# Two norms per token tile shared by VectorE and ScalarE, three tile splits moved to VectorE, four table loads placed early

## The chip, the cores and the metric

The kernel runs on one core of a Trainium2 chip. The metric is the device time of one execution in microseconds (us), taken as the median of several. The core has five engines that run their own instruction streams and meet only at semaphores: TensorE (PE, matmuls and transposes into PSUM), VectorE (DVE), ScalarE (ACT), GpSimd (POOL) and SyncE (SP), which here only issues weight loads by DMA.

## The reference

Two transformer blocks on 256 tokens of width 1024, float32. What matters here are the places where a residual stream `x` is normalised, and what follows each.

```python
# block 1
x = layer_norm(ALPHA * x + g1 * mix) * ln1_g + ln1_b
h = layer_norm(x) * (1.0 + sc2) + sh2
ffn = moe_ffn(h, ...)        # router: sigmoid scores, top 8 of 64 experts; 38 expert steps
x = layer_norm(ALPHA * x + g2 * ffn) * ln2_g + ln2_b
# block 2, two layers
h = _rmsnorm(x, mix_norm[0]); x = x + _fox_pool_mixer(h, ...)
x = x + _swiglu(_rmsnorm(x, ffn_norm[0]), ...)
h = _rmsnorm(x, mix_norm[1]); x = x + _rwkv7_time_mix(h, ...)
x = x + _swiglu(_rmsnorm(x, ffn_norm[1]), ...)
```

## The kernel before

The 256 tokens are two tiles of 128 partitions (`NT = 2`, t = 0 and 1). `x` and `h_tok` hold both as 128 x 2 x 1024. Weights come as 1 MB tiles of 128 x 2048 through a ring of 6 slots, issued in order by SP (L588); each load waits until PE has used the slot's last tile. A product is done in three float32r matmuls (L809 to L811): ACT rounds a tile to its high part (`round_tile`, L1598, semaphore `w_hi`), and DVE or POOL subtracts it to get the rest in `ring_lo` (`rest_of_tile` on DVE, L2075; `rest_of_tiles` on POOL, L638; semaphore `w_split`). Only then may PE use the tile.

The order on every engine is the order of the program text, written out by hand. `Steps` makes an instruction wait for the one ahead of it on its own engine. What an engine waits for it waits for in order, so an instruction behind a wait is late with it.

Norms: `layer_norm` (L2035) and `rms_norm` (L2044) on DVE take bn_stats of two halves and bn_aggr per token tile, ask ACT for the square roots of both tiles at once (`root(2)`, L1626 to L1630, semaphores `root_asked` and `root_done`), take the reciprocal (L2016), and scale both tiles (L2042, or L2051 and L2052). An affine `x * gain + bias` runs over both tiles at once (L2348, L2349 after `w_o`, L2467, L2468 after the experts). Then PE transposes `h_tok` (`turn_all`, `turn_half`, L890), ACT writes the high part of the transposed rows (`hT_parts`, L1615 or L1618), and DVE the rest (L2098 or L2101). The stages named after the transposes are h2T (into the router), a0T (first mixer), f0T (first feed-forward), r0T (second mixer) and f1T (second feed-forward).

Router: PE multiplies by `router_w` (`stack`, L874), ACT copies the partial sums (`stacked_sums`, L1624), PE adds them (`stack_sums`, L863), ACT takes the Sigmoid (L1828) after it has rounded the last of the three tiles of the shared expert ("moe", 2), and DVE sorts out the top 8 (L2361 to L2385). POOL makes the rests of the three "moe" tiles. `placed` on DVE then works out which expert sits where (L2124 to L2166); at its first `tables` (L2141) POOL issues the first indirect loads of expert weights (L705, L709), and later gathers the tokens' rows of `h2_rows` (L697). `mod_gate_half` (L2068) copies the gate of the second half to SBUF on DVE. `routed` on PE runs the 38 expert steps (L1041 transposes, L1055 gate and up, L1074 down, L1088 combine).

## Time and profile before

| | |
|---|---|
| runs (us) | 1967.17, 1970.4, 1979.52; median 1970.4 |
| profiled execution | 1973.28 us, of it 1971.5 us from first to last instruction |
| PE busy | 1778.5 us (90%), granted clock 0.947 on average |
| DVE / ACT / POOL busy | 930.2 / 644.8 / 519.9 us |
| chain that ended last | PE 76%, DVE 11%, DMA 7%, ACT 3%, issue 3%, POOL 1% |

The chain that ended last is followed back from the last instruction, at each step to what released it. So DVE is busy for 47% of the time but only 11% of the span hangs on it. Most of that 11% lies in the short stretches between two products, where a norm must be finished before PE has work again. All times below are us from the start of the span, unless marked otherwise.

### The profile page before, as it was taken

To read this page: it belongs to the slowest core of one execution; us is meant where nothing else is said; L and a number is where in the kernel's file an instruction comes from. 1 tells how busy PE (TensorE), PEld (TensorE's weight loads), DVE (VectorE), ACT (ScalarE), POOL (GpSimd) and SP (SyncE) were. 2 spreads that over 40 slices of the span, in tenths; PEclk is the share of its full clock that TensorE was granted. 3 is DMA by queue.
4 is the path that set the end of the run, shared out by engine and by line. 5 is a ranking of instruction groups with operands and counts; after the bars stand their busy time and mean duration, and the time that the engine had idled before them with its cause. 6 is when DMAs were issued, how large, how long until landed. Compare 5 with 4: busy or idle time off the path is not lost.

```text
span 1971.5 us, 29696 instructions
## 1 busy us (share of the span) xinstructions
PE 1778.5 (90%) x12406; PEld 1277.0 (65%) x12406; DVE 930.2 (47%) x1355; ACT 644.8 (33%) x863; POOL 519.9 (26%) x372
## 2 busy tenths in 40 slices
PE   5989998999779999999999498889997979979998
PEld 2889996795534344444444276678886749857887
DVE  4286626677612121222222664455447765665453
ACT  3444345241202111111111234343434352324442
POOL 0278888100434445354543000000000002200000
PEclk9999999899879999999999688889998989989999
DMA  9445551167599998979897432155553400023442
GB/s 360 179 150 193 181 185 42 65 237 283 221 423 423 416 384 312 390 295 397 329 380 311 180 128 86 64 187 192 191 190 133 168 22 25 3 70 143 183 183 104
DMA packets 64970, 414.40 MB, mean 210 GB/s; under 512 B 20613, under 2 KB 20629, under 8 KB 24529
## 3 DMA queue, kind: packets, MB, share of 16 engines
q0 software_dynamic: 37808, 218.05, 27.5%
q1 hardware_dynamic: 26624, 192.95, 26.4%
q8 instruction: 92, 1.51, 0.3%
q10 hardware_dynamic: 416, 1.66, 0.2%
q14 instruction: 30, 0.24, 0.0%
HBM read 550.99 MB, written 2.10 MB: 281 GB/s over the span
## 4 chain that ended last, share of the span: by engine, by line
PE 76%; DVE 11%; DMA 7%; ACT 3%; issue 3%; POOL 1%; DVEq 0%; POOLq 0%; ACTq 0%; SPq 0%
PE ps L1055 12%; PE ps L809 10%; PE ps L810 10%; PE ps L811 10%; PE ps L1074 6%; PE ps L845 4%; PE ps L846 4%; PE ps L847 4%; PE ps L1088 3%; PE ps L1413 2%; PE ps L863 1%; PE ps L1041 1%; DMA ring<-in_moe_dn,arena 1%; DMA arena<-in_moe_dn,arena 1%; PE ps L1449 1%
## 5 line engine op out<-in xcount | busy, mean ns | idle before, releaser
L810 PE MATMUL ps<-ring_lo,arena_r 128*128 128x512 f32 x888 | 356.0, 401 | 0.0
L1055 PE MATMUL ps<-arena 128*32 128x512 f32 (+2 forms) x832 | 244.4, 601 | 7.5 <-DMA spare<-in_moe_gu,arena 3.9
L809 PE MATMUL ps<-arena_r 128*128 128x512 f32 x528 | 211.4, 400 | 7.0 <-DVE arena_r L2101 7.0
L847 PE MATMUL ps<-arena_r,ring_lo 128*128 128x256 f32 x768 | 215.7, 281 | 0.0
L811 PE MATMUL ps<-arena_r 128*128 128x512 f32 x528 | 207.7, 393 | 0.0
L1055 PE MATMUL ps<-ring,arena 128*32 128x512 f32 (+2 forms) x560 | 201.5, 601 | 4.9 <-issue 2.1
L810 PEld LDWEIGHTS ps<-ring_lo,arena_r 128*128 128x128 f32 x888 | 171.4, 193 | 35.6
L2075 DVE TENSOR_TENSOR ring_lo<-ring,arena_r 128x2048 fp32r<-128x2048 f32 x66 | 150.7, 2291 | 77.6 <-ACT arena_r L1598 77.5
L638 POOL TENSOR_TENSOR ring_lo<-ring,high 128x2048 fp32r<-128x2048 f32 x28 | 128.5, 4591 | 132.9 <-ACT high L1598 132.9
L1598 ACT ACTIVATE high<-ring 128x2048 fp32r<-128x2048 f32 x62 | 118.4, 1917 | 125.1 <-PE ps L845 67.7
L845 PE MATMUL ps<-arena_r,high 128*128 128x256 f32 x528 | 151.3, 287 | 3.0 <-DVE ring_lo L2075 1.4
L2446 DVE SCALAR_TENSOR_TENSOR arena<-ps,arena 128x256 f32<-128x256 f32 x38 | 18.4, 484 | 277.4 <-ACT arena L1699 277.4
L846 PE MATMUL ps<-arena_r,high 128*128 128x256 f32 x528 | 149.1, 282 | 0.0
L847 PEld LDWEIGHTS ps<-arena_r,ring_lo 128*128 128x128 f32 x768 | 145.7, 190 | 0.0
L1598 ACT ACTIVATE arena_r<-ring 128x2048 fp32r<-128x2048 f32 x66 | 126.1, 1919 | 38.6 <-DMA ring<-in_weights 38.6
L1055 PEld LDWEIGHTS ps<-arena 128*32 128x32 f32 (+2 forms) x832 | 75.6, 126 | 77.9 <-issue 77.8
L1074 PE MATMUL ps<-arena 128*32 128x512 f32 (+2 forms) x416 | 123.9, 596 | 0.5 <-ACT arena L1707 0.5
L890 PE MATMUL ps<-cst,arena 128*128 128x128 f32 x372 | 63.4, 318 | 65.9 <-DVE arena L2052 34.1
L1055 PE MATMUL ps<-spare,arena 128*32 128x512 f32 (+1 forms) x272 | 121.5, 600 | 0.6
L809 PEld LDWEIGHTS ps<-arena_r 128*128 128x128 f32 x528 | 100.2, 190 | 27.2 <-issue 7.6
L811 PEld LDWEIGHTS ps<-arena_r 128*128 128x128 f32 x528 | 100.2, 190 | 21.3
L845 PEld LDWEIGHTS ps<-arena_r,high 128*128 128x128 f32 x528 | 100.1, 190 | 6.8 <-issue 2.7
(451 smaller groups left out, 3559.5 us busy)
## 6 DMA issues: line engine op xcount, KB each, us to landing
ring<-in_weights SPq DMA_DIRECT2D x183, 1024.0 KB, 4.8
arena<-in_ln POOLq DMA_DIRECT2D x2, 1024.0 KB, 7.5
arena<-in_lora POOLq DMA_DIRECT2D x1, 1152.0 KB, 5.5
arena<-in_x POOLq DMA_DIRECT2D x1, 1024.0 KB, 12.7
h_rows<-arena ACTq DMA_DIRECT2D x1, 1024.0 KB, 11.0
arena<-in_bands POOLq DMA_DIRECT2D x1, 1024.0 KB, 11.8
arena<-in_rw_kk_ka POOLq DMA_DIRECT2D x2, 512.0 KB, 7.3
arena<-in_rw_w0a POOLq DMA_DIRECT2D x1, 1024.0 KB, 4.8
```

The source lines that it names most:

```text
L638: pool.tensor_tensor(ring_lo[:, s, :], ring[:, s, :], hi_of(stage, i).bitcast(F32), ALU.subtract).then_inc(sem(f"w_split{s}"), 1)
L809: head = pe.matmul(dst, hi, w, start=start, stop=False, skip_group_check=True)
L810: pe.matmul(dst, hi, rest, start=False, stop=False, skip_group_check=True)
L811: return head, pe.matmul(dst, lo, w, start=False, stop=stop, skip_group_check=True)
L845: head = pe.matmul(dst, w, hi[:, k, :], start=(k == 0), stop=False)
L846: pe.matmul(dst, w, lo[:, k, :], start=False, stop=False)
L847: mm = pe.matmul(dst, rest, hi[:, k, :], start=False, stop=(k == count - 1))
L890: mm = pe.transpose(pb(stage, unit)[0:src.shape[1], n * P:n * P + src.shape[0]], src, ident)
L1055: mm = pe.matmul(pb("moe", mu("gu", i))[at, :], x_cols[:, k, at], gu_w[s % SETS][:, k * 512:(k + 1) * 512], start=(k == 0), stop=(k == KC ...
L1074: mm = pe.matmul(pb("moe", mu("y", i, n))[at, :], hid_cols[:, i % 2, f, at], dn_w[s % SETS][:, f * D + n * 512:f * D + n * 512 + 512], sta ...
L1598: fn(hi_of(stage, i), ring[:, s, :], ACT.Copy).then_inc(sem(f"w_hi{s}"), 1)
L2075: tt(ring_lo[:, s, :], ring[:, s, :], hi_of(stage, i).bitcast(F32), S).then_inc(sem(f"w_split{s}"), 1)
```

## The change

- The norms go by token tile. After `w_o` and after the experts, DVE asks for tile 0's root as soon as its moments are known (`ask_deviation`), ACT takes it (`root(1, t)`), DVE writes 1/deviation and -mean/deviation (`centre`), and ACT normalises the tile in place with one ACTIVATE with a scale and a bias per partition (`centred_rows`, semaphore `scaled`). Gain, bias and moments run on DVE per tile (`norm_with_gain`).
- Of each following norm into `h_tok`, ACT scales tile 0 (`scaled_rows`) and DVE tile 1 (`rms_of_second`). PE transposes tile 0 as soon as ACT has it (`turn_tile(stage, 0)`), tile 1 after DVE. This holds for a0T, f0T, r0T and f1T; h2T is turned as before.
- The rests of the three "moe" tiles leave POOL for DVE, tiles 0 and 1 ahead of the top-8 search and tile 2 behind it, ahead of `placed`. The copies of `mod_gate` go from DVE to ACT.
- ACT rounds tile ("moe", 2) after the router's Sigmoid. The rest of ("hy_in", 1) moves on DVE from ahead of the norm after the experts to behind it, and ACT rounds ("hy_in", 0) one step earlier.
- `warm(func)` is an ACTIVATE on one column. It makes the compiler put the table load of `func` there: Sigmoid at the router, Exp ahead of the copies of `qkT`, Tanh, Sigmoid and Exp in the second mixer.

```diff
 @@ POOL
             row(buf(7), a["ln1"]).then_inc(sem("ln_in"), 16)
-            rest_of_tiles("moe", 3)
 @@ PE (the same for f0T, r0T, f1T with scaled 7, 8, 9)
+            pe.wait_ge(sem("scaled"), 6)
+            turn_tile("a0T", 0)
             pe.wait_ge(sem("a0_ready"), 1)
-            turn_all("a0T", h_tok, KC)
+            turn_tile("a0T", 1)
 @@ ACT
+            def centred_rows(t):
+                scales[0] += 1
+                act.wait_ge(sem("scale_ready"), scales[0])
+                fn(x[:, t, :], x[:, t, :], ACT.Identity, bias=sml("ms", 1, t),
+                   scale=sml("rs", 1, t)).then_inc(sem("scaled"), 1)
+            def scaled_rows(shifted=False):
...
+                    ins = fn(h_tok[:, 0, :], x[:, 0, :], ACT.Copy, scale=sml("rs", 1))
+                ins.then_inc(sem("scaled"), 1)
+            def warm(func):
+                step(fn(sml("warm", 1), sml("one", 1), func))
...
+                round_tile("hy_in", 0)
                 y_rounded(STEPS - 1)
-                round_tiles("hy_in", 0, 1)
+                round_tile("hy_in", 1)
...
+            root(1, 0)
+            centred_rows(0)
             partial_sums("ada2", 0)
-            root(2)
-            partial_sums("ada2", 1, 2)
-            root(2)
+            root(1, 1)
+            centred_rows(1)
+            partial_sums("ada2", 1)
+            root(1, 0)
+            scaled_rows(shifted=True)
+            partial_sums("ada2", 2)
+            root(1, 1)
             partial_sums("ada2", 3)
...
             stacked_sums("router")
-            round_tile("moe", 2)
+            warm(ACT.Sigmoid)
+            for u in range(2):
+                full(act, "gate2", 2 * u + 1)
+                step.read(fn(mod_gate[:, u * 512:(u + 1) * 512], pb("gate2", 2 * u + 1), ACT.Copy), "gate2", 2 * u + 1)
             for t in range(NT):
                 full(act, "router", 1 + t)
                 step.read(fn(rt_scores[:, t, :], pb("router", 1 + t)[:, 0:EXPERTS], ACT.Sigmoid), "router", 1 + t)
+            round_tile("moe", 2)
...
-            root(2)
+            root(1, 0)
+            scaled_rows()
+            root(1, 1)
             hT_parts("f0T", p2("ffn_norm", 8))
 @@ DVE
+            def norm_with_gain(gain, bias, name, ask, answer):
+                for t in range(NT):
+                    scaled_seen[0] += 1
+                    dve.wait_ge(sem("scaled"), scaled_seen[0])
+                    step(tt(x[:, t, :], x[:, t, :], gain, M))
+                    if t == 0:
+                        centre(1)
+                    else:
+                        answer()
+                        scaled_seen[0] += 1
+                    step(tt(x[:, t, :], x[:, t, :], bias, A), name if t else None)
+                    for half in range(2):
+                        half_moments(x, t, half)
+                    if t == 0:
+                        ask(0)
...
             hT_parts("h2T")
-            for u in range(2):
-                mod_gate_half("gate2", u, u)
+            rest_of_tiles("moe", 0, 1)
...
             step(tt(flat(picked), above, masked, ALU.not_equal), "marks")
+            rest_of_tile("moe", 2)
             experts("moe")
...
-            rest_of_tiles("hy_in", 0, 1)
+            rest_of_tile("hy_in", 0)
...
-            rms_norm(h_tok, x, "a0_ready")
+            norm_with_gain(buf(0)[:, 0:D], buf(0)[:, D:2 * D], "x2_ready", ask_rms, rms_of_first)
+            rms_of_second("a0_ready")
+            rest_of_tile("hy_in", 1)
```

How the instructions stand on ACT at the router, before: the row of L1624 is just ahead of these.

```order
L1598 ACTIVATE twin_r<-ring 128x2048 [waits w_loaded2,ps_read3]
L1828 ACT_TABLE_LOAD
L1828 ACTIVATE arena<-ps 128x64 [waits ps_full4]
L1828 ACTIVATE arena<-ps 128x64 [waits ps_full5,ps_read4]
L1637 ACT_TABLE_LOAD [waits gu_full0]
L1637 ACTIVATE arena<-ps 128x256 [waits ps_read5]
```

And of the change, on the same engine and place (its own line numbers: L1672 is `warm`, L1877 the copies of `mod_gate`, L1880 the Sigmoid, L1617 the rounding, L1679 the Silu of the shared expert):

```order
L1672 ACT_TABLE_LOAD
L1672 ACTIVATE small<-small 128x1 [waits ps_read3]
L1877 ACTIVATE arena<-ps 128x512 [waits ps_full4,act_order]
L1877 ACTIVATE arena<-ps 128x512 [waits ps_full6,ps_read4]
L1880 ACTIVATE arena<-ps 128x64 [waits ps_full4,ps_read6]
L1880 ACTIVATE arena<-ps 128x64 [waits ps_full5,ps_read4]
L1617 ACTIVATE twin_r<-ring 128x2048 [waits w_loaded2,ps_read5]
L1679 ACT_TABLE_LOAD
L1679 ACTIVATE arena<-ps 128x256 [waits gu_full0]
```

The Sigmoid no longer stands behind the rounding that waits for the weight tile, and the Silu's table load no longer carries the wait for PE.

On DVE between the last expert step and the first moments, before (L2433 ends the last step's masks, L2461 is the first work on the experts' sum):

```order
L2433 TENSOR_SCALAR last_r<-arena 128x128 x2
L2075 TENSOR_TENSOR ring_lo<-ring,high 128x2048 [waits w_hi3]
L2075 TENSOR_TENSOR ring_lo<-ring,high 128x2048 [waits w_hi4]
L2461 TENSOR_TENSOR arena<-ps,arena 128x512 [waits combined]
L2461 TENSOR_TENSOR arena<-ps,arena 128x512 [waits dve_order]
```

The same place in the change:

```order
L2540 TENSOR_SCALAR last_r<-arena 128x128 x2
L2177 TENSOR_TENSOR ring_lo<-ring,high 128x2048 [waits w_hi3]
L2570 TENSOR_TENSOR arena<-ps,arena 128x512 [waits combined,ps_read6,ps_read4]
L2570 TENSOR_TENSOR arena<-ps,arena 128x512 [waits dve_order]
L2573 SCALAR_TENSOR_TENSOR arena<-arena 128x1024 [waits dve_order]
```

One of the two rests has left this place; it stands behind `a0_ready` now.

## Rows read from the trace of the kernel before

**Rows 1.** The waits of PE: engine line waited for, us in total, times, longest.
```profile
PE ps L890 <- DVE arena L2052: 34.1, 3, 25.0
```

**Rows 2.** Stretches: PE, PEld, DVE, ACT, POOL busy (x count), granted clock, DMA share, GB/s.
```profile
545.00:559.00 14.00, 2.81 (x14) 2.66 (x14) 0.40 (x2) 0.00 (x0) 3.95 (x4) 0.50 1.01 421
559.00:1101.00 542.00, 527.32 (x3179) 239.76 (x3177) 114.94 (x231) 100.67 (x192) 229.05 (x232) 0.99 0.91 364
```

**Rows 3.** DVE's timeline behind `w_o`: start, us, line, form, idle before and releaser.
```profile
472.32 0.69 DVE L2343 TENSOR_TENSOR arena<-ps,arena 128x512 f32<-128x512 f32 x1 [0.41 <-PE ps L811]
488.17 1.23 DVE L2061 SCALAR_TENSOR_TENSOR arena<-ps,arena 128x1024 f32<-128x1024 f32 x1
```

**Rows 4.** ACT's timeline at the router and the shared expert.
```profile
501.34 0.38 ACT L1624 ACTIVATE arena<-ps 128x256 f32<-128x256 f32 x1
503.67 1.91 ACT L1598 ACTIVATE twin_r<-ring 128x2048 fp32r<-128x2048 f32 x1 [1.94 <-DMA ring<-in_weights]
505.60 1.28 ACT L1828 ACT_TABLE_LOAD   x1
516.08 1.28 ACT L1637 ACT_TABLE_LOAD   x1 [8.71 <-PE ps L811]
```

**Rows 5.** DVE's timeline in the top-8 search.
```profile
507.46 1.31 DVE L2361 TENSOR_TENSOR arena<-arena 128x128 f32<-128x128 f32 x1 [3.45 <-ACT arena L1828]
508.81 3.23 DVE L2363 MAX8 arena<-arena 128x8 f32<-128x8 f32 x16
512.08 1.17 DVE L2364 TENSOR_TENSOR arena<-arena 128x16 f32<-128x16 f32 x1
513.29 0.29 DVE L2372 TENSOR_TENSOR arena<-arena 128x128 f32<-128x128 f32 x1
```

**Rows 6.** POOL's timeline: the three rests, then the first load of expert weights.
```profile
499.62 9.00 POOL L638 TENSOR_TENSOR ring_lo<-ring,high 128x2048 fp32r<-128x2048 f32 x2 [50.47 <-ACT high L1598]
508.59 4.62 POOL L638 TENSOR_TENSOR ring_lo<-ring,twin_r 128x2048 fp32r<-128x2048 f32 x1
523.14 1.06 POOL L705 DMA_INDIRECT ring<-in_moe_gu,arena  x1 [9.93 <-DVE arena L2141]
```

**Rows 7.** The chain that ended last, at the gather: start, us, what.
```profile
541.09 17.32 DMA arena<-h_rows,arena
558.46 1.97 PE ps L1041 x8
```

**Rows 8.** DVE's timeline behind the experts.
```profile
1099.60 4.49 DVE L2075 TENSOR_TENSOR ring_lo<-ring,high 128x2048 fp32r<-128x2048 f32 x2 [0.72 <-ACT high L1598]
1104.01 1.41 DVE L2461 TENSOR_TENSOR arena<-ps,arena 128x512 f32<-128x512 f32 x2
1115.23 2.29 DVE L2467 TENSOR_TENSOR arena<-arena 128x2048 f32<-128x2048 f32 x1
1125.23 0.75 DVE L2052 TENSOR_SCALAR arena<-arena,small 128x1024 f32<-128x1024 f32 x1
```

**Rows 9.** DVE behind `hy_out`, then ACT at f0T and at the second mixer.
```profile
1280.55 0.69 DVE L2547 TENSOR_TENSOR arena<-ps,arena 128x512 f32<-128x512 f32 x1 [1.15 <-PE ps L811]
1284.21 0.75 DVE L2052 TENSOR_SCALAR arena<-arena,small 128x1024 f32<-128x1024 f32 x1
...
1286.23 3.22 ACT L1618 ACTIVATE arena_r<-ps,small 128x256 fp32r<-128x256 f32 x8 [3.11 <-PE ps L890]
...
1498.20 1.06 ACT L1901 ACTIVATE arena_r<-arena 128x1024 fp32r<-128x1024 f32 x1 [3.69 <-DVE arena L2588]
```

**Rows 10.** DVE's timeline behind r0T.
```profile
1489.85 1.22 DVE L2572 TENSOR_TENSOR arena<-arena 128x1020 f32<-128x1020 f32 x1 [0.83 <-ACT arena L1588]
```

**Rows 11.** ACT's timeline at two table loads for Exp, and the copies ahead of one.
```profile
1200.99 2.49 ACT L1581 ACTIVATE arena<-ps 128x512 f32<-128x512 f32 x4
1207.54 1.28 ACT L1870 ACT_TABLE_LOAD   x1 [4.06 <-DVE small L2515]
...
1603.03 1.28 ACT L1934 ACT_TABLE_LOAD   x1 [6.47 <-DVE arena L2633]
```

117 lines of the change are left out of this document (90 added, 27 removed).

## Prediction

> **What bounds the kernel now.** I read the busy shares first, then the waits of PE, then the chain that ended last, and then the timelines of DVE, ACT and POOL in each stretch that the diff touches. PE is busy for 90% of the span, so only stretches in which PE has nothing to do can pay. In the 38 expert steps it has almost none: 527 us of matmuls in 542 us at full clock, with the DMA engines 91% busy beside it [rows 2]. That stretch should move as a block. PE's largest wait is for the second scaling of a norm, 34.1 us in three waits, 25.0 of them behind the experts [rows 1]. The changed stretches are eight: `w_o` to the router, the router to the first gather, the experts' end to a0T, the attention's start, f0T, r0T, the Exp in the second mixer, and f1T. The sum is made stretch by stretch, against the profiled execution of 1973.28 us. It lies 2.9 us above the median of the runs, 1970.4.
>
> **Prices.** A DVE instruction costs its duration and about 0.03 us. A 128 x 2048 tensor_tensor takes 2.29 us [rows 8], half of it 1.22 [rows 10], a tiny one about 0.2 with its gap (estimate: the 0.29 of 128 elements [rows 5] less its length). No instruction before normalises 1024 columns on ACT. Its nearest row is a plain Copy of 1024 columns, 1.06 us [rows 9]. Above, the bound is the 1.91 us of a 2048 column rounding [rows 4]. I take 1.06, since the shape is the same. DVE does a tile in 0.75 [rows 8].
>
> **1. `w_o` to the router: 0.7 us.** Before, the modulation of `ada2` starts at 488.17, 15.85 us after the last product piece at 472.32 [rows 3]. In the new order DVE loses two whole-tile scalings per norm half to ACT and one exposed root, but gains 5 tiny instructions. Walked through by the prices, the modulation starts at 486.4, 1.8 us earlier. Not all of it gets through. ACT must round the weight tiles ("moe", 0) and ("moe", 1) ahead of `stacked_sums`, and the tile after them is only there at 503.67, after ACT had waited 1.94 us for it [rows 4]. Loads come back to back here, so tile 1 is about one load and half the `h2_rows` store earlier, near 499, and its rounding ends near 500.8. `stacked_sums` then starts at about 500.7 and not at 501.34 [rows 4], which leaves 0.6 to 0.7. Bounds: 0 if the tile is later, 1.8 if not in the way.
>
> **2. The router: 3.0 us more.** Before: rounding from 503.67 to 505.58, table load to 506.88, two Sigmoids, DVE starts at 507.46 [rows 4, 5]. New: `stacked_sums` ends at 501.1, load 1.28, warm 0.2, two gate copies of 0.6 (the chained 0.62 of a 512 column copy [rows 11]), Sigmoids 0.5: DVE starts at 504.5, so 2.96 earlier, the 0.7 of step 1 among it. Then DVE's two small tensor_tensors took 1.31 and 1.17 us where the same form with 128 elements takes 0.29. The first ended at 508.77 and the second at 513.25, when POOL's rests ended at 508.62 and 513.21 [rows 5, 6]. The 16 MAX8, with one input each, were not held. With the rests gone from POOL, I credit 1.0 and 0.9. Bounds 0 and 1.9. So the search ends 4.9 us earlier. Against that, the rest of ("moe", 2), 2.29 us like L2467 [rows 8], stands ahead of `placed`. Before, DVE sat about 1 us here until PE had counted. PE itself starts the shared expert 2.9 us earlier. `placed` starts 3.7 us earlier by this: 2.96 + 1.9, less 2.3, plus the 1 us of sitting and 0.1. The Silu's load (1.28 behind a wait of 8.71 [rows 4]) now lies in the slack and pays nothing, as the rest covers it. If that rest were quicker, it would pay up to 1.3.
>
> POOL's first indirect load, at 523.14, waits for DVE L2141 [rows 6], which is in `placed`. The gather is issued at 541.09 and its rows land 17.3 us later, at 558.4 [rows 7], with the DMA full at 421 GB/s [rows 2]: it lies behind four sets of expert weights. Hence it lands 3.7 us earlier exactly if the first load is issued 3.7 us earlier. **Steps 1 and 2: 3.7 us** of the start of the expert steps.
>
> **3. Behind the experts: 4.0 us.** PE's last combine ends at 1101.04 (the modelled end). DVE starts on it only at 1104.01, behind two rests from 1099.60 [rows 8]. With one rest left it starts at 1101.2: 2.8. From there to `a0_ready` it was 21.97 us (1104.01 to 1125.98 [rows 8]). By tile: two products and a scaling of x 2.72, moments 1.70, ask 0.2, products 1.46, centre 0.4, 1.26, 1.70, 0.2; then gain 1.26, centre 0.4, bias 1.26, 1.70, 0.4; 1.26, 0.2, 1.26, 1.70; 0.4, root 0.3, reciprocal 0.2, scaling 0.78. Together 20.8: 1.2 saved. The norm saves so little because two scalings, 1.7 us, and one exposed root, 0.8, leave DVE, while the splitting adds tiny instructions. PE has turned tile 0 meanwhile. Unit 0 of a0T is complete two transposes after `a0_ready` instead of four, about 0.45 at low clock; but the moved rest, 2.3 us, delays DVE's half of a0T by that much again. With it in between, DVE's half comes about as much later as the earlier transposes bring, so the 0.45 is not counted. Total 2.8 + 1.2 = 4.0.
>
> **4. Attention: 0.2 us lost.** The load at 1207.54 sat behind a wait of 4.06 and was exposed, 1.28. But the warm Exp now stands ahead of the four `qkT` copies, which run back to back from 1200.99 [rows 11] and which PE waits for. It costs 1.28 and 0.2 there. The load is moved from one place on the path to another.
>
> **5. f0T and f1T: 1.3 us each.** The last piece starts at 1280.55, `f0_ready` is at 1284.96, ACT's first hT at 1286.23 [rows 9]. New: 0.72, reciprocal 0.2, 0.73, 0.24, 0.4, root 0.3, 0.2, 0.78 gives `f0_ready` at 1284.15, 0.8 earlier; ACT's tile 0 is done at 1282.6. Unit 0 needs two transposes less after it, 0.45. With `f1_ready` the rows repeat. **r0T: 0.3**, since the rounding of ("rw_r", 2) and its rest still lie ahead of L2572, which waited only 0.83 for ACT [rows 10].
>
> **6. Exp in the second mixer: 1.3 us.** The load at 1603.03 is exposed behind a wait of 6.47 [rows 11]. ACT is idle ahead of it, so warming hides all 1.28. The loads for Tanh and Sigmoid are not waited for: the products behind them wait for a later one.
>
> Sum: 3.7 + 4.0 - 0.2 + 2.6 + 0.3 + 1.3 = **11.7 us**, 1973.3 becomes 1961.6, and the median 1970.4 becomes **1958.7**.
>
> The Trainium skill (ScalarE: Activation LUTs, What ACT_TABLE_LOAD costs) adds a drain and puts each switch at about 2.66 us. By it step 6 would be worth 2.66 and step 4 would still about cancel, a sum of 13.1 and 1957.3. The trace shows the next ACTIVATE right behind the 1.28, so I keep 1.28. The same page (Rules for kernel authors) sends adds and multiplies to VectorE, against this change. By it ACT's tile would be the last one, which is the third rival.
>
> **The rivals.**
> - Forecast, chance 0.60: 1958.7, own range 1955 to 1963 (step 1 from 0 to 1.8, the port from 0 to 1.9, each step's latencies).
> - The router's gain stays out, 0.18. The search is sooner, but `placed` is held by the rest of ("moe", 2), or that tile lands later as the `h2_rows` store now shares its DMA time. For: DMA full until 503.7, 2.29 us ahead of `placed`. Against: 5 us between its landing and its use. Steps 1 and 2 give 0 to 1: 11.7 - 3.2 = 8.5, 1961.9.
> - ACT's tile is the last, 0.10. If a per-partition ACTIVATE of 1024 takes the upper bound, 1.91, it is 0.85 longer. There are eight such on ACT, and at about four of them DVE has no work of its own left to cover it: 3.4 lost, 1962.1.
> - Slower, 0.04: PE's clock. It was granted at half before the first gather, 0.50 [rows 2], after PE had sat idle. If at the six restarts it stays at the low level (1.2 GHz) longer, every us of it costs half a us of matmuls. It decides from 23 us more of low clock, 4 us per restart. With 8 us per restart it would be 24 - 11.7 = 12.3 slower: 1982.7. Against: the gaps get shorter, not longer.
> - Large gain, 0.05: the waits in the expert steps, 14.7 us of 542 [rows 2], shrink with the new phase of loads by 8 or more: 1950.
> - It changes nothing, 0.03: every gain is given back in the 14.7 us of waits: 1970.
>
> **How the numbers follow.** 1% is 19.7 us, about what a measurement of this kernel can tell from no change. Only the large gain with all else at its upper bound passes it, and the clock must take 31 us to pass on the other side. Faster 0.05, same 0.92, slower 0.03. The forecast, the router's and ACT's rivals hold 0.88. The range over them, widened for the runs' own scatter (the median lies 3 above the lowest run, 9 below the highest), is 1952 to 1967.5.
>
> **What would show it.** In the changed profile: the first Sigmoid at about 504, not 506.9; L2361's and L2364's counterparts at 0.3 each; POOL's first indirect load near 519.4; PE's first expert transposes near 554.7; DVE's first work on the experts' sum within 0.3 us of PE's end; `a0_ready` 20.8 us after it; first ACT hT at f0T 4.4 us after the last piece, not 5.7; the Exp at the second mixer with no load ahead; `qkT` copies 1.5 us later. It is wrong if the small tensor_tensors stay at 1.2 without POOL, if an ACTIVATE of 1024 takes 1.5 or more, or if the expert steps take longer than 542 us.

## The result, and the profile after

The changed kernel takes 1957.46 us (median of 17 runs), the kernel before 1970.49 us beside it. The ratio is 0.9933, with a 95% interval from 0.9919 to 0.9948: 13.2 us less, between 10.2 and 16.0. The forecast was 11.7 us less and 1958.7 us. The profiled execution spans 1955.7 us, 15.8 less than the 1971.5 of before.

So the number came out. The reasons did so only in part, and the stages show where. The table cuts the span at marks that every kernel here has (an instruction on DVE, or the first matmul of a product on PE), so each row is the difference of two start times read from the timelines. "Last piece" is the last tensor_tensor in which DVE adds a product's result.

| stretch (us) | before | change | difference | forecast |
|---|---|---|---|---|
| start to the last `w_o` piece (unchanged code) | 472.32 | 476.22 | +3.90 | 0 |
| to the first tensor_tensor of the top-8 search | 35.14 | 34.01 | -1.13 | -3.0 |
| to `placed` | 11.19 | 10.09 | -1.10 | -0.7 |
| to PE's first expert transposes | 39.81 | 39.99 | +0.18 | 0 |
| to PE's last combine | 542.19 | 538.43 | -3.76 | 0 |
| to DVE's first work on the experts' sum | 3.36 | 0.53 | -2.83 | -2.8 |
| to PE's first matmul behind a0T | 28.73 | 27.48 | -1.25 | -1.2 |
| to the last q/k piece on ACT | 67.62 | 66.63 | -0.99 | 0 |
| attention, to the last `hy_out` piece | 80.19 | 75.95 | -4.24 | +0.2 |
| f0T, to the first product | 11.58 | 10.33 | -1.25 | -1.3 |
| to the feed-forward's last piece | 190.05 | 189.35 | -0.70 | 0 |
| r0T, to the first product | 14.16 | 13.08 | -1.08 | -0.3 |
| to DVE's last LoRA sums (L2633) | 105.90 | 106.87 | +0.97 | 0 |
| the Exp, to DVE's next instruction | 7.23 | 5.94 | -1.29 | -1.3 |
| to the last `rw_o` piece | 157.68 | 156.45 | -1.23 | 0 |
| f1T, to the first product | 11.31 | 10.31 | -1.00 | -1.3 |
| to the end | 193.04 | 194.04 | +1.00 | 0 |

Six rows (the experts' end, the norm behind it, f0T, r0T, the Exp, f1T) hold little but work that the change moved, and sum to 8.7 us. The two rows at the router (to the search and to `placed`) are the change's too, 2.2 us more. The largest rows, +3.90, -3.76 and -4.24, lie where I had forecast nothing or next to nothing. Whether the code makes them, one pair of profiles can't tell.

The page of the changed kernel: busy times, and three groups of PE's waits (engine line, releaser: us in total, times, longest). Compare [rows 1].

```profile
PE 1774.3 (91%) x12406; PEld 1270.9 (65%) x12406; DVE 929.4 (48%) x1370; ACT 657.8 (34%) x886; POOL 506.5 (26%) x369
```

```profile
PE ps L904 <- ACT arena L1667: 22.1, 3, 17.5
PE ps L861 <- ACT arena L1877: 3.5, 1, 3.5
PE ps L904 <- DVE arena L2135: 3.0, 3, 1.5
```

The wait of 25.0 us behind the experts has become 17.5 us for ACT's tile 0 and 1.5 for DVE's tile 1. The second row is new: PE's router sums (L861) wait 3.5 us for ACT's copy of `mod_gate`.

ACT's timeline at the router in the change (start, us, line, form, idle before and releaser), to be held against [rows 4].

```profile
500.54 1.91 ACT L1617 ACTIVATE high<-ring 128x2048 fp32r<-128x2048 f32 x1 [0.90 <-DMA ring<-in_weights]
504.32 1.91 ACT L1617 ACTIVATE high<-ring 128x2048 fp32r<-128x2048 f32 x1 [1.87 <-DMA ring<-in_weights]
506.14 0.37 ACT L1643 ACTIVATE arena<-ps 128x256 f32<-128x256 f32 x1
506.52 1.28 ACT L1672 ACT_TABLE_LOAD   x1
508.05 1.23 ACT L1877 ACTIVATE arena<-ps 128x512 f32<-128x512 f32 x2
509.55 0.22 ACT L1880 ACTIVATE arena<-ps 128x64 f32<-128x64 f32 x1 [0.27 <-PE ps L861]
```

The Sigmoid no longer waits for tile ("moe", 2), but it waits for tile ("moe", 1). Here and below a tile counts as landed when ACT starts to round it. That is 28.1 us behind the last `w_o` piece (504.32 less 476.22). Then the load, the warm instruction and the first copy stand ahead of PE's sums.

DVE's timeline in the change: the search, and the stretch behind the experts. Compare [rows 5, 8].

```profile
510.23 0.29 DVE L2467 TENSOR_TENSOR arena<-arena 128x128 f32<-128x128 f32 x1 [1.67 <-ACT arena L1880]
510.55 3.24 DVE L2469 MAX8 arena<-arena 128x8 f32<-128x8 f32 x16
513.83 0.19 DVE L2470 TENSOR_TENSOR arena<-arena 128x16 f32<-128x16 f32 x1
...
1099.27 1.42 DVE L2570 TENSOR_TENSOR arena<-ps,arena 128x512 f32<-128x512 f32 x2
...
1119.28 0.75 DVE L2135 TENSOR_SCALAR arena<-arena,small 128x1024 f32<-128x1024 f32 x1
1120.06 2.29 DVE L2177 TENSOR_TENSOR ring_lo<-ring,high 128x2048 fp32r<-128x2048 f32 x1
1122.27 4.11 DVE L2203 SCALAR_TENSOR_TENSOR arena_r<-ps,small,arena_r 128x256 fp32r<-128x256 f32 x8
```

The two small tensor_tensors take 0.29 and 0.19 us, not 1.31 and 1.17. Behind the experts `a0_ready` falls at 1120.03, which is 20.76 us after DVE's start at 1099.27. The forecast had 20.8.

### The profile page after: what moved, and what is told of

Read it like the earlier page. It is cut to its first block, busy times and chain, and to the rows that moved or that the text cites. A ratio compares the mean times of both kernels' runs of the same rounds, so it can differ in the third digit from the quotient of the medians.

```text
span 1955.7 us, 29751 instructions
## 1 busy us (share of the span) xinstructions
PE 1774.3 (91%) x12406; PEld 1270.9 (65%) x12406; DVE 929.4 (48%) x1370; ACT 657.8 (34%) x886; POOL 506.5 (26%) x369
## 3 DMA queue, kind: packets, MB, share of 16 engines
q1 hardware_dynamic: 26624, 192.95, 26.7%
## 4 chain that ended last, share of the span: by engine, by line
PE 76%; DVE 11%; DMA 7%; issue 3%; ACT 3%; POOL 1%; DVEq 0%; POOLq 0%; ACTq 0%
PE ps L1066 12%; PE ps L807 10%; PE ps L808 10%; PE ps L809 10%; PE ps L1085 6%; PE ps L845 4%; PE ps L843 4%; PE ps L844 4%; PE ps L1099 3%; PE ps L1430 3%; PE ps L861 2%; PE ps L1052 1%; DMA ring<-in_moe_dn,arena 1%; DMA arena<-in_moe_dn,arena 1%; PE ps L1466 1%
## 5 line engine op out<-in xcount | busy, mean ns | idle before, releaser
L1617 ACT ACTIVATE high<-ring 128x2048 fp32r<-128x2048 f32 x62 | 118.6, 1916 | 128.4 <-PE ps L843 67.6
L638 POOL TENSOR_TENSOR ring_lo<-ring,high 128x2048 fp32r<-128x2048 f32 x26 | 119.6, 4604 | 82.8 <-ACT high L1617 82.8
L1617 ACT ACTIVATE arena_r<-ring 128x2048 fp32r<-128x2048 f32 x66 | 126.1, 1920 | 38.5 <-DMA ring<-in_weights 38.5
L2177 DVE TENSOR_TENSOR ring_lo<-ring,high 128x2048 fp32r<-128x2048 f32 x36 | 82.3, 2292 | 55.7 <-ACT high L1617 55.2
L1741 ACT ACTIVATE arena<-ps 128x256 f32<-128x256 f32 x38 | 14.6, 384 | 269.0 <-PE ps L1066 269.0
```

Source lines behind the costliest of these rows:

```text
L638: pool.tensor_tensor(ring_lo[:, s, :], ring[:, s, :], hi_of(stage, i).bitcast(F32), ALU.subtract).then_inc(sem(f"w_split{s}"), 1)
L1617: fn(hi_of(stage, i), ring[:, s, :], ACT.Copy).then_inc(sem(f"w_hi{s}"), 1)
L2177: tt(ring_lo[:, s, :], ring[:, s, :], hi_of(stage, i).bitcast(F32), S).then_inc(sem(f"w_split{s}"), 1)
```

## The experiments

All kernels are timed against the kernel before on the same chip. Ratios have a 95% interval. A difference of 1 to 3 us is below what a median tells here (the intervals are 5 to 16 us wide), so what a run decides is read from its stages. A granted clock of 1.00 is TensorE's 2.4 GHz, 0.50 is 1.2 GHz, called half clock here.

### What holds the router: copies of `mod_gate` back on DVE

```diff
 @@ ACT
-            for u in range(2):
-                full(act, "gate2", 2 * u + 1)
-                step.read(fn(mod_gate[:, u * 512:(u + 1) * 512], pb("gate2", 2 * u + 1), ACT.Copy), "gate2", 2 * u + 1)
 @@ DVE
-            rest_of_tiles("moe", 0, 1)
+            rest_of_tile("moe", 0)
+            for u in range(2):
+                mod_gate_half("gate2", u, u)
+            rest_of_tile("moe", 1)
```

> The changed kernel, but the two copies of mod_gate are made by DVE again, between the rests of tiles (moe, 0) and (moe, 1). Measure: from the last w_o piece on DVE to the first tensor_tensor of the top-8 search, 35.14 us before and 34.01 in the change, where I had forecast 32.2. Theory 1 (the copies hold the router): in the change PE's router sums wait 3.51 us for the second... the first copy of mod_gate on ACT, which stands behind the Sigmoid's table load (1.28) and the warm instruction (0.20), since both use one PSUM bank. With the copies on DVE the sums run beside the load, and the search starts when the load and the rest of (moe, 1) end: 1.6 us sooner, 32.4 us, and the first indirect load of POOL and PE's first expert transposes come sooner by 1.4 to 1.7. Theory 2 (only the landing of weight tile (moe, 1), 28.1 us behind the last w_o piece, holds the router): 34.0 again, nothing moves. Total: 1.5 us, below what five rounds can tell.

Measured: from the last `w_o` piece to the search 32.10 us, 1.9 less than in the change. From there to PE's expert transposes 50.1, as in the change. Ratio to the kernel before 0.9936 (0.9911 to 0.9960), so the total doesn't show it. PE's timeline of this kernel at the router sums and the shared expert:

```profile
502.36 0.66 PE L861 MATMUL ps<-cst,arena 128*128 128x64 f32 x4 [0.27 <-ACT arena L1643]
504.80 0.77 PE L807 MATMUL ps<-high,arena_r 128*128 128x512 f32 x1 [1.78 <-ACT arena L1877]
```

The sums wait 0.27 us for `stacked_sums` and no longer 3.51 for a copy behind the load. In the change that wait is in this row:

```profile
508.79 1.09 PE L861 MATMUL ps<-cst,arena 128*128 128x64 f32 x4 [3.51 <-ACT arena L1877]
```

Theory 1 holds: my forecast had priced the two copies as 1.2 us of ACT time, and not seen that they stand behind the table load on PE's way to the Sigmoid. But not all of the 1.9 us are the copies', since tile ("moe", 1) came 1.0 us sooner in this profile (27.1 us behind the last `w_o` piece, not 28.1). Counted from that tile's rounding, the search starts 5.6 to 6.0 us later in the five kernels with the copies on ACT. With the copies on DVE and a tile as late (28.0 and 29.6 us, two kernels below) it starts 4.2 us later, which is ACT's 1.91 and DVE's 2.29 for that tile. So the copies are worth 1.4 to 1.7 us where the tile is late.

### DVE and POOL: rests back on POOL, and rests on DVE in the kernel before

```diff
 @@ POOL
+            rest_of_tiles("moe", 3)
 @@ DVE
-            rest_of_tiles("moe", 0, 1)
...
-            rest_of_tile("moe", 2)
```

> The changed kernel, but POOL makes the rests of the three moe tiles again. Measure: the two small tensor_tensors of the top-8 search, 1.31 and 1.17 us before, 0.29 and 0.19 in the change. Theory 1 (DVE and POOL hold each other up): POOL's rests run beside the search, and one or both take over 1 us again, where a rest runs beside them; the MAX8 between them stay at 3.2 for 16. Theory 2 (something else of the change made them short, such as the place of the Sigmoid): 0.3 and 0.2. The first indirect load moves little either way: 2 us of such delays against 2.29 us of the rest of (moe, 2) which no longer stands ahead of placed.

Ratio 0.9958 (0.9935 to 0.9981), median 1963.75. From the last `w_o` piece to PE's expert transposes it took 87.5 us, where four profiles with the change's router took 83.8 to 85.1: on the mean 1.3 more up to the search, since the weight tile came late (29.7 us), and 1.8 more from there to `placed`. DVE's and POOL's timelines of this kernel:

```profile
508.16 1.34 DVE L2468 TENSOR_TENSOR arena<-arena 128x128 f32<-128x128 f32 x1 [12.52 <-ACT arena L1882]
509.53 3.23 DVE L2470 MAX8 arena<-arena 128x8 f32<-128x8 f32 x16
512.80 1.91 DVE L2471 TENSOR_TENSOR arena<-arena 128x16 f32<-128x16 f32 x1
```

```profile
500.38 8.97 POOL L638 TENSOR_TENSOR ring_lo<-ring,high 128x2048 fp32r<-128x2048 f32 x2 [51.03 <-ACT high L1619]
510.09 4.58 POOL L638 TENSOR_TENSOR ring_lo<-ring,twin_r 128x2048 fp32r<-128x2048 f32 x1 [0.75 <-ACT twin_r L1619]
```

Each held instruction ends 0.04 to 0.16 us after a POOL instruction: 509.50 after 509.35, 514.71 after 514.67. The MAX8 between, with one input, isn't held, though POOL's third rest starts beside it. How much is lost depends on the moment. In the kernel before with an early Exp (below), the third rest started 0.03 us ahead of the search. Its DVE and POOL timelines:

```profile
511.95 4.68 DVE L2366 TENSOR_TENSOR arena<-arena 128x128 f32<-128x128 f32 x1 [4.58 <-ACT arena L1832]
```

```profile
511.92 4.55 POOL L638 TENSOR_TENSOR ring_lo<-ring,twin_r 128x2048 fp32r<-128x2048 f32 x1
```

Here 0.29 us of work took 4.68, `placed` began 14.42 us after the search's start and not 11.19, and from `w_o` to PE's expert transposes it was 92.13 us, 6 more than the 86.14 of the first profile. Of these 6 us 3.2 lie between the search and `placed`, the others ahead of and behind it. So theory 1 of the experiment with POOL's rests holds: DVE and POOL hold each other up. The Trainium skill (SBUF — State Buffer, SBUF: two separate sides) says that VectorE and GpSimd share a port pair, and that of an instruction of VectorE with two SBUF inputs and one of GpSimd that reads SBUF, the one that starts first locks the other out for its whole length. By that rule, the traces agree: 0.64 to 4.68 us where POOL's rest was under way, 0.29 and 0.19 where it wasn't.

Then the same alone in the kernel before (tile 0's rest ahead of the `mod_gate` copies, tile 1's behind, tile 2's ahead of `placed`):

> The kernel before, with one thing of the change: DVE makes the rests of the three moe tiles, (0) ahead of the two copies of mod_gate, (1) behind them, (2) ahead of placed. In the profiles so far the first small tensor_tensor of the search took 1.31, 1.34 and 4.68 us and the second 1.17, 1.91 and 0.19 us wherever POOL made the rests (before, the change with POOL rests, before with the early Exp), and 0.29 and 0.19 wherever DVE made them; undoing the DVE rests in the change took the median from 1957.5 to 1963.8. Measure: the two durations, the time from the last w_o piece to PE's first expert transposes (86.1, 87.5 and 92.1 us in those three), and the median. Theory 1 (the delay by POOL is the larger part of what the router gives, and is larger on average than the 2.5 us of the profile of before): 0.3 and 0.2 us, the stage takes 84 to 86 us, and the median falls by 3 to 6 us. Theory 2 (my forecast: 1.9 us of delay against 2.29 us of the rest ahead of placed): the stage 85 to 86 us and the median the same within 1 us.

The two took 0.29 and 0.19 us, the stage to PE's expert transposes 86.62 us, against 86.14 and 86.66 in the two profiles of the kernel before in which the delay was small. Ratio 1.0000 (0.9975 to 1.0025). So theory 2: what the port gives back, the rest of ("moe", 2) ahead of `placed` takes. What remains is that the bad case of 92 can't occur. How often it occurs in the kernel before, three profiles don't tell.

### The attention: where the Exp's load stands

One place in the change, moved behind the copies:

```diff
 @@ ACT
-            warm(ACT.Exp)
             copy_units("qkT", 4, lambda i: buf(10)[:, i * 512:(i + 1) * 512])
+            warm(ACT.Exp)
```

> The changed kernel, but the warm Exp stands behind the four qkT copies instead of ahead of them. Measure: from the last q/k piece that ACT copies (L1913 of the change) to the last hy_out piece on DVE: 80.2 us before, 75.95 in the change, where I had forecast 80.4. Theory 1 (latency only): the copies start 1.48 us sooner and the load stays hidden in ACT's wait of about 5 us, so 74.5 us, and PE's wait ahead of the first logits is 1.7 instead of 3.2 us. Theory 2 (the clock decides): in the change the granted clock falls to half in PE's 3.2 us wait and is back 9 us later, before the loop over the heads is under way; before the change it stayed full there and fell in the next wait (2.4 us), and was half from 1209 to 1222.5. With the shorter first wait the fall comes later, inside the loop, and the stage is 76 to 79 us although the copies are sooner.

And in the kernel before, the warm Exp ahead of the copies, as the change has it:

> The kernel before, with one thing of the change: the warm Exp ahead of the qkT copies. Measure: from the last q/k piece that ACT copies to the last hy_out piece, 80.2 us before. Theory 1 (my forecast, latency only): the load moves from one place on the path to another, 80.4 us. Theory 2 (the clock): the wait of PE ahead of the first logits grows from 1.7 to 3.2 us, the clock falls there and is back before the loop over the heads is under way, and the stage takes about 76 us as in the change. If it takes 80, the 4.2 us came from something else of the change, or from chance.

Ratios: 0.9899 (0.9863 to 0.9936) for the late one in the change, 0.9983 (0.9959 to 1.0006) for the early one in the kernel before. The stage from the last q/k piece to the last `hy_out` piece, in all profiles of this study, with PE's busy time at half clock in it (windows of 2 us, PE's busy time in each times twice the share of the clock that was missing):

| Exp's load | stage (us) | of it half clock (us) |
|---|---|---|
| exposed in the loop (before, and two experiments on it) | 80.2, 75.6, 77.6 | 26.5, 15.9, 21.6 |
| ahead of the copies (change twice, three experiments on it, one on before) | 76.0, 77.6, 78.6, 76.0, 77.6, 77.5 | 17.8, 22.2, 22.9, 18.0, 22.0, 21.9 |
| behind the copies (five kernels) | 73.4, 73.1, 71.5, 73.5, 73.2 | 14.1, 16.3, 9.7, 14.0, 16.5 |

The stretches of the attention in three kernels, and in a fourth further down: PE, PEld, DVE, ACT, POOL busy (x count), granted clock, DMA share, GB/s. First the kernel before.

```profile
1200.99:1209.00 8.01, 4.89 (x26) 3.17 (x24) 2.80 (x7) 3.83 (x6) 0.00 (x0) 1.00 0.35 131
1209.00:1222.50 13.50, 12.48 (x39) 9.20 (x40) 4.96 (x16) 5.12 (x18) 0.00 (x0) 0.51 0.01 1
```

The change:

```profile
1195.52:1197.50 1.98, 0.00 (x0) 0.00 (x0) 0.00 (x0) 1.88 (x4) 0.00 (x0) 0.94 0.99 418
1197.50:1206.80 9.30, 8.55 (x21) 5.31 (x22) 2.74 (x7) 1.60 (x5) 0.00 (x0) 0.50 0.01 4
```

The change with the Exp behind the copies:

```profile
1190.81:1218.00 27.19, 22.48 (x128) 16.04 (x127) 15.61 (x46) 14.48 (x40) 0.00 (x0) 1.00 0.11 39
```

Before, the clock fell inside the loop over the heads, behind PE's wait for the exposed load. In the change it fell one wait sooner, where the warm Exp had made that wait 3.2 us instead of 1.7. With the load behind the copies both waits are short (1.7 and 1.1 us), and here the clock stays full for 27 us, into the loop. That is so in three of the five kernels with the late load. In the other two, the combined one and the last one below, the clock fell all the same, for 6.8 us from 5.2 and 5.5 us behind the last q/k piece, after the same 1.7 us of waiting. The combined kernel:

```profile
1198.50:1205.30 6.80, 6.80 (x19) 4.43 (x19) 3.14 (x8) 2.19 (x9) 0.00 (x0) 0.50 0.00 1
```

So with the short waits the first fall is spared or 6.8 us long, and the length of the waits alone does not settle which. In the kernels with the exposed or the early load it came each time and lasted 6.8 to 13.7 us.

So the -4.24 us of the first pair of profiles is not the early Exp's merit: means are 77.8 us where the load is exposed (75.6 to 80.2), 77.2 with the early warm (76.0 to 78.6), 72.9 with the late one (71.5 to 73.5). The first two can't be told apart, and the 77.5 of the early warm in the kernel before decides for neither theory of that run: it lies between its two values and among the others. The forecast of about nothing stands, for a reason that I had not named. My theory 2 of the late Exp (the fall comes later and costs more) is refuted, and theory 1 had the 1.5 us but not the 3 more of the clock. The relation is plain in the table: from 9.7 to 26.5 us of half clock the stage grows by 8.7, about half a us for each. The late load's gain shows in the total too: 0.9899 is the lowest ratio of any kernel here without the idle transposes of the last experiments.

### The experts' end: one rest moved in the kernel before

```diff
 @@ ACT
-                y_rounded(STEPS - 1)
-                round_tiles("hy_in", 0, 1)
+                round_tile("hy_in", 0)
+                y_rounded(STEPS - 1)
+                round_tile("hy_in", 1)
 @@ DVE
-            rest_of_tiles("hy_in", 0, 1)
+            rest_of_tile("hy_in", 0)
...
             rms_norm(h_tok, x, "a0_ready")
+            rest_of_tile("hy_in", 1)
```

> The kernel before, with one thing of the change: the rest of (hy_in, 1) stands behind the scaling into h_tok and no longer ahead of the merge of the experts' sum, and ACT rounds (hy_in, 0) a place earlier. Measure: from PE's last combine to DVE's first work on the sum (3.36 us before, counted from the start of the last matmul; 0.53 in the change), and from that to PE's first stack matmul behind a0T (28.7 before, 27.5 in the change). Theory (the forecast's step 3): 0.5 for the first, 2.8 us sooner; the second grows by the moved rest less what hid it, to 30.5 to 31, since here all of the transposes come behind a0_ready and DVE's half of a0T would stand right behind them; so of the 2.8 us 0.5 to 1 stay in the first product's start, if the rest is in the way, and all 2.8 if PE's 3.7 us of transposes cover it. This kernel has the attention of before unchanged: its stage from the last q/k piece to the last hy_out piece was 80.2 us in the one profile of before; if clock chance made that, it may come out between 76 and 80 here.

From PE's last combine to DVE's first work on the sum: 0.43 us instead of 3.36. From there to the first matmul behind a0T 28.69, and 28.72 to 28.74 in three profiles of kernels with both rests in the old place. So all of the 2.9 us stay, and the moved rest costs nothing behind `a0_ready`: PE needs 3.7 us for its transposes at half clock, and the 2.29 fit beside them. That part of my expectation (0.5 to 1 us lost) was wrong. The norm by tile, the rest of what the change does there, then gives the 1.25 us more, the same in every profile with it and the rest in this place (27.46 to 27.49). Ratio 0.9995 (0.9968 to 1.0022): a gain of 3 us that the median does not show.

### f1T: what the clock takes back

The norm ahead of f1T as before (one root for both tiles, both scalings on DVE, `turn_all`), all else as in the change.

> The changed kernel with the norm ahead of f1T as before: one root for both tiles, both scalings on DVE, all transposes behind it. Measure: from the last rw_o piece to the first product of the feed-forward (11.31 us before and 10.31 to 10.66 in the change), and from there to the end (192.8 to 193.0 before, 193.9 to 194.0 in the change). Theory 1 (the clock takes the gain back): PE's transposes by tile leave it at half clock 1.5 to 2 us longer in the feed-forward, so with this norm undone the first part is 11.3 and the second 193.0, and the sum is the same 204.3. Theory 2 (the feed-forward got slower for another reason of the change): 11.3 and 194.0, sum 205.3.

Ratio 0.9957 (0.9932 to 0.9982). f1T took 11.31 us and the rest to the end 193.49, the sum 204.8: between the theories. The first 8 us of the last feed-forward, in the kernel before, the change, and this one (columns as above, the clock is third from the end):

```profile
1778.46:1786.46 8.00, 8.00 (x28) 6.42 (x29) 4.24 (x3) 3.15 (x4) 0.00 (x0) 0.79 0.00 0
```

```profile
1761.66:1769.66 8.00, 8.00 (x24) 6.33 (x25) 3.90 (x2) 2.22 (x2) 0.00 (x0) 0.65 0.00 0
```

```profile
1769.71:1777.71 8.00, 8.00 (x26) 6.43 (x27) 4.03 (x2) 2.66 (x3) 0.00 (x0) 0.72 0.00 0
```

In 8 us the clock was half for 3.4, 5.6 and 4.5 us (twice the missing share). Take half a us of lost work for each from the time to the end: 193.04 less 1.7 is 191.3, 194.04 less 2.8 is 191.2, 193.49 less 2.25 is 191.2. The feed-forward itself is the same in all three, and the clock alone makes the difference. The kernels with a full clock there, below, bear it out: they take 191.3 us. So theory 1 is right about the cause. It is not right about the amount, since undoing the norm brought back half of it, not all. In the seven profiles with the norm by tile and no fill the sum of f1T and what follows is 204.2 to 204.6, in the four of the kernel before and what was made from it 204.0 to 204.4. Nothing is won at f1T. That the one profile with this norm undone lies 0.2 to 0.7 us above all of these is left open.

### Chance and code: the change again, and repairs together

> The changed kernel as it is, for a second profile and for the median beside the two below on one chip. If the stages are a matter of the code, from the last w_o piece to PE's first expert transposes it is 84 to 85 us, merge to the first product behind a0T 27.5, f0T 10.3, r0T 13.1, the Exp stretch of the second mixer 5.9, f1T 10.3 and behind it 193.9. What differs more than 0.3 us from the first profile (I expect the experts by up to 3 us, the attention by up to 3 us, and the start up to w_o by up to 8) is chance, and should go with the time at half clock in it.

Median 1962.3, ratio 0.9941 (0.9919 to 0.9963). The own stretches repeat within 0.06 us (27.49 behind the experts, 10.33 at f0T, 13.08 at r0T, 5.93 at the Exp, 10.37 at f1T) or 0.3 us (193.85 behind f1T, 83.8 from `w_o` to PE's expert transposes). Others do not. The experts took 541.4 us and not 538.4. The start up to `w_o` was 474.96 here and ranged from 468.3 to 476.3 over all profiles, with the same code in it. That scatter does go with the clock, as I had expected: TensorE was granted half clock for 13.7 us of the start in the three profiles of 468.3 to 468.5, and for 30.7 us in the five above 475.2. So the +3.90 of the first table is chance. The experts ranged from 538.0 to 544.3 in the change and the kernels made from it, and from 539.6 to 542.2 in the kernel before and those made from it. The two overlap, so the -3.76 is not shown to be the code's. With the clock it does not go: 538.4 and 541.4 us had 8.9 and 8.1 us at half.

Then three repairs together: the `mod_gate` copies on DVE, the Exp behind the copies, the rest of ("hy_in", 1) behind DVE's half of a0T.

> The changed kernel with three repairs: the copies of mod_gate on DVE, the warm Exp behind the qkT copies, and the rest of (hy_in, 1) behind DVE's half of a0T. From the profiles so far: 1.9 us at the router, 1.5 to 2.5 in the attention, and up to 0.6 at a0T, where DVE's half started 1122.27 with ACT's first two pieces done 0.5 to 0.6 us before. Theory 1 (the gains add up): 4 to 5 us under the change, a median near 1953. Theory 2 (only the attention counts, and the router's gain is lost in the loads of the expert steps): 1955.

Ratio 0.9912 (0.9882 to 0.9941), median 1955.44. The stages: 33.86 to the search (the weight tile landed late), 27.05 behind the experts (0.43 less), 73.1 in the attention. Behind the experts and in the attention the repairs hold by stage. At the router this profile has only 0.5 us of the 1.9 (83.9 us to PE's expert transposes against 84.4 in the change), but the two others with the copies on DVE and the last rest in its old place have 2.1 (82.2 and 82.4). The median is the 1955 of theory 2, yet the stages do not bear out its reason, that the router's gain is lost. By the ratios the total is 4 to 6 us better than the change's, with intervals that overlap, and no better than the late Exp's load alone (0.9899).

On top of it, the rest of ("moe", 2) inside `placed`:

```diff
-            rest_of_tile("moe", 2)
             experts("moe")
...
+                rest_of_tile("moe", 2)
                 dve.wait_ge(sem("slots"), 4)
```

> The combined kernel of the run before (mod_gate on DVE, warm Exp late, rest of (hy_in, 1) late), and DVE makes the rest of (moe, 2) inside placed, ahead of its wait for PE's fourth result (1.1 us), and no longer ahead of it. Theory 1 (the first indirect load sets when the tokens' rows land: from it to PE's first expert transposes it was 35.3 to 35.6 us in all nine profiles): PE counts at about 1.6 us behind the search's end, so placed starts 0.9 us sooner, and so do the first indirect load and the transposes: 83.0 us from the last w_o piece instead of 83.9, with 35.5 unchanged. Theory 2 (the gather's own issue, 18 us behind the first load and held by DVE, sets it): the rest delays DVE by 1.2 to 2.3 us in between, so the 35.5 grow to 36.5 to 37.5 and the stage is 84.2 to 85.

From search to `placed` 9.17 us instead of 10.07, from there to PE's expert transposes 39.8 and not longer: theory 1. Ratio 0.9918 (0.9889 to 0.9948), median 1955.96: the total doesn't tell it from the one before. On the same chip the change itself took 1962.3, so all the repairs together are worth 6.3 us there. Over all profiles it was 35.3 to 35.8 us from the first indirect load to the first expert transposes, whatever DVE did in between. The prediction's assumption that this time is fixed held.

### PE kept busy in its waits

If the time at half clock is what separates these kernels, then giving PE something to do should pay more than a faster norm. `fill` is so many transposes of the identity into a PSUM bank that nobody reads (shown here at f1T, added in the same way at a0T, f0T and r0T):

```diff
+            def fill(n, dst):
+                for _ in range(n):
+                    pe.transpose(dst[:, 0:P], ident, ident)
...
+            claim(pe, "f1T", 0)
+            fill(12, pb("f1T", 0))
             pe.wait_ge(sem("scaled"), 9)
             turn_tile("f1T", 0)
             pe.wait_ge(sem("f1_ready"), 1)
             turn_tile("f1T", 1)
+            fill(28, pb("rw_o", 0))
```

> The combined kernel of the run before, and PE makes transposes of the identity that nobody reads while it waits: 110 ahead of a0T and 24 behind it, 12 and 28 at f0T, 20 and 48 at r0T, 12 and 28 at f1T (0.12 us each at full clock, 0.24 at half). Theory 1 (the low clock behind these places comes from PE's waits): the granted clock stays at 1.00 there, the product times behind lose what half clock cost them: f1T to the end 191.3 instead of 193.8 us, f0T to the end of the feed-forward 188 instead of 189.8, and the stretch behind f1T's last piece 9.7 instead of 10.6, since PE's own transposes take 2 us and not 3.7. In all 6 to 9 us. Theory 2 (such small work does not keep the clock up, or the fall has another cause): the clock falls as before, the fills take twice the time and end up to 2 us behind what PE waits for, and the kernel is 3 to 6 us slower than the combined one.

Median 1947.16, ratio 0.9881 (0.9853 to 0.9908), 8.8 us under the kernel without fills on the same chip (1955.96). From f1T to the end 191.36 us, and f1T itself 9.88. At a0T, f0T and r0T the clock still fell. PE's timeline of this kernel at f0T:

```profile
1264.79 3.22 PE L913 MATMUL ps<-cst 128*128 128x128 f32 x28
1270.13 0.47 PE L807 MATMUL ps<-arena_r 128*128 128x512 f32 x1 [2.12 <-DVE arena_r L2215]
```

2.1 us stayed open there, and the clock fell 0.8 us after the products had begun. So the last run fills longer:

> The kernel with PE's idle transposes once more, longer, and with the rest of (moe, 2) inside placed: 150 and 34 transposes at a0T (110 and 24 in the run before), 12 and 42 at f0T (28), 20 and 70 at r0T (48), 12 and 42 at f1T (28). In the run before the clock stayed at 1.00 at f1T, where 2.1 us of PE's wait were left open, but fell at f0T (2.1 us open) and at r0T (3.3 us), and at a0T (5.5 us). Theory 1 (the open rest of the wait lets it fall): with 0.3 to 0.6 us left open it stays full there too, f0T to the end of the feed-forward 188.0 instead of 189.6 us, r0T to the second mixer's sums 104.2 instead of 105.8, f1T to the end 191.4 again, and the first transposes of a0T take 1.1 us and not 1.97; with the 0.9 us of placed, 4 to 5 us in all, a median of 1942 to 1943. Theory 2 (the waits ahead of the transposes, 1 to 1.6 us, or chance decide): f0T and r0T stay at 189.6 and 105.8, and the median at 1946 to 1947.

Median 1943.09, ratio 0.9851 (0.9812 to 0.9891). The wait behind the transposes of f0T, first in the combined kernel without fills, then in this one:

```profile
1276.51 0.77 PE L807 MATMUL ps<-arena_r 128*128 128x512 f32 x1 [4.55 <-DVE arena_r L2200]
```

```profile
1265.33 4.75 PE L913 MATMUL ps<-cst 128*128 128x128 f32 x42
1270.67 0.47 PE L807 MATMUL ps<-arena_r 128*128 128x512 f32 x1 [0.59 <-issue]
```

At f1T 0.55 us stayed open, at r0T 0.89. The first 8 us of the products behind f0T and r0T, in this kernel:

```profile
1270.67:1278.67 8.00, 8.00 (x35) 6.63 (x36) 4.36 (x4) 4.37 (x4) 0.00 (x0) 1.00 0.43 144
1471.68:1479.68 8.00, 8.00 (x34) 6.47 (x35) 6.41 (x13) 2.12 (x2) 0.00 (x0) 1.00 0.14 33
```

The same two in the combined kernel without fills:

```profile
1276.51:1284.51 8.00, 8.00 (x27) 6.47 (x28) 3.86 (x3) 2.60 (x4) 0.00 (x0) 0.76 0.43 137
```

```profile
1479.39:1487.39 8.00, 8.00 (x23) 6.33 (x24) 6.41 (x13) 2.12 (x2) 0.00 (x0) 0.64 0.00 0
```

The feed-forward takes 187.94 us (189.80 without fills), the stretch behind r0T 104.48 (107.12), the last feed-forward with its tail 191.28 (193.75). PE is busy for the whole 8 us in all four rows, but gets 35 and 34 instructions into them and not 27 and 23. That is 7.0 us less at three places, where I had expected 188.0, 104.2 and 191.4. All three lie below every profile without fills (189.3 to 190.3, 105.8 to 107.3, 192.7 to 194.0).

Two things more belong to the account. Behind the Exp of the second mixer, in code without fills, the two kernels with them took 158.5 and 158.0 us, where all others took 156.4 to 157.7, and PE was busy at half clock for 19.5 and 19.9 us there instead of 13.8 to 18.6. So 0.9 to 1.7 us of the gain are lost again; why the clock is low for longer there, no run shows. At a0T it overshot: 34 transposes at half clock took 5.58 us, and the first matmul came 1.0 us late (28.09 us). But the stretch behind it, up to the last q/k piece, took 64.2 us in both kernels with fills, with 3.4 us at half clock, and 66.7 and 66.8 us in the two that they were made from. In that stretch (the combined kernel, then this one):

```profile
1126.55:1193.29 66.74, 63.27 (x279) 49.11 (x280) 43.72 (x57) 28.48 (x27) 0.00 (x0) 0.92 0.39 142
```

```profile
1123.35:1187.52 64.17, 60.68 (x280) 47.84 (x280) 42.73 (x57) 28.47 (x27) 0.00 (x0) 0.97 0.42 148
```

One kernel without fills had 64.4 us there, with 3.5 at half, so this part is likely but not shown. Theory 1 holds at f0T, r0T and f1T, and this is the best kernel of the study, 29 us (21 to 37) under the one before. Its interval overlaps that of the run before, so the step between the two rests on the stages.

## Why the prediction was right, and where it was not

**The total.** 1958.7 was forecast and 1957.46 measured, in the range and within 1% of before. Of the 13.2 us by the ratio, the change's own stretches carry 10 to 12: 2.0 at the router (84.4 us, the mean of four profiles with the change's router, against 86.1 and 86.7, leaving the 92.1 out; 3.9 with it), 2.83 and 1.25 behind the experts, 1.25 at f0T, 1.08 at r0T, 1.29 at the Exp, 0.6 in the attention, nothing at f1T. Part of what is left is in unchanged code and goes with the clock: behind the Exp 157.1 to 157.7 us became 156.4 to 157.1, while 15.6 to 18.6 us of PE's busy time at half clock became 13.8 to 15.3 (the kernel before and three made from it, the change twice and six made from it).

That the total fits so well is in part luck. The router and f1T were put 3.0 us too high (3.7 for 2.0, 1.3 for nothing), r0T and the attention 1.6 too low, and 1 to 3 us of the measured gain lie outside of the change's own stretches.

**Step 1, right in its walk and wrong in its neighbour.** The modulation starts 14.01 us behind the last product piece, by my walk 14.1. But I had tile ("moe", 1) "near 499", 26.7 us behind that piece. It came 28.1 behind, and between 27.1 and 29.7 in the other profiles. It looks like my second rival's mechanism ("that tile lands later as the `h2_rows` store now shares its DMA time"), at another tile than I named, since the store is issued 19.1 us behind the piece and not 20.9. But the tile is as late without it: in the three kernels made from the one before, with the store at 20.9, it is rounded 28.1, 28.4 and 28.6 us behind the piece, after ACT had waited 0.9 to 1.4 us for it. Of the profiles of the kernel before and what was made from it, only the one that I had read had it by 27.1. So what failed is the reading of the tile's time from one profile. What sets that time was not tried.

**Step 2, two terms mis-sized.** Forecast 3.0 us sooner for the search, measured 1.1. 1.4 us are tile 1's landing, the rest the waits of PE and ACT on each other, which the chain "load, warm, copies, Sigmoids" had as pure sum (501.1 to 504.5 is 3.4 us, though the terms named give only 3.2; measured 3.7). The copies belong elsewhere altogether: on DVE the search is 1.4 to 1.9 us sooner. The port's term (1.0 and 0.9 us) was right by size for those rows, and too small for the kernel before at its worst: three profiles with the old order lost 2.0, 1.3 and 4.4 us.

**Step 3, right twice.** 2.83 for 2.8 and 1.25 for 1.2. The 0.45 at the transposes was rightly left out: with the moved rest behind DVE's half of a0T it comes back (27.05 against 27.48).

**Step 4, right by chance.** Forecast +0.2. The load's move costs not 1.5 but 2.5 to 3.2 us up to DVE's first logits, since the first logits run at half clock in part or in whole, and gives that back in the loop. On the mean of the profiles it is 0.6 us less, which is within their scatter.

**Step 5.** f0T 1.25 for 1.3. f1T 1.00 for 1.3, but all of it is lost again in the feed-forward. That is the fourth rival, PE's clock, which I had set against "the gaps get shorter, not longer". They do, and the clock still stays low 2.2 us longer in the first 8 us of the feed-forward. Behind f0T it did not cost that: the feed-forward took 189.3 to 190.3 us with the norm by tile and no fills, and 189.7 to 190.1 without. r0T 1.08 for 0.3: DVE's wait of 0.83 for ACT's copy [rows 10] is gone, since PE turns tile 0 sooner, and ACT's copies begin 4.19 instead of 5.57 us behind the last piece. I had seen the wait and not taken it.

**Step 6.** 1.29 for 1.3, and the same in every later profile within 0.01 us. The 2.66 us for a switch, by which this step would have been worth twice that, was not seen. The Tanh's and the first Sigmoid's load hide nothing, as said: 43.76 us from the norm's reduce to L2633 in both kernels.

**The third rival** (ACT's tile is the last) did not come: an ACTIVATE of 1024 with a scale took 1.15 us and with scale and bias 1.24, not 1.91. Behind the experts DVE waits for none of them. ACT's rows there:

```profile
1105.77 1.24 ACT L1657 ACTIVATE arena<-arena,small 128x1024 f32<-128x1024 f32 x1 [1.70 <-DVE small L2122]
1115.43 1.15 ACT L1667 ACTIVATE arena<-arena,small 128x1024 f32<-128x1024 f32 x1 [1.32 <-DVE small L2129]
```

## What to carry to other kernels

Where PE is busy for 90% and waits in a few places, read the granted clock behind each wait before pricing a faster norm: here 1 us won ahead of a product was lost in it. Idle transposes that filled the waits gave 7.0 us at f0T, r0T and f1T, less 1 to 2 us behind them, and the norms by tile 2.3. Look at what shares a PSUM bank (the memory that matmuls write) with an instruction that is moved behind a table load, and put a load where its engine already waits, not ahead of copies that PE waits for. When stages scatter by 3 us with unchanged code, two profiles agree with nearly any theory, so judge an edit by its own stretch in several kernels.
